# Feed-forward of the first block: six more pairs of the first linear in seven block products, 19 of 22 per layer

## What is computed

```python
def conv_ffn(h, in_w, conv_w, conv_b, out_w):
    u = causal_dwconv(h @ in_w, conv_w, conv_b)   # in_w 1024 x 5632, conv of width 3 over positions
    g, v = jnp.split(u, 2, axis=-1)
    return (jax.nn.silu(g) * v) @ out_w           # out_w 2816 x 1024
```

## Time and profile before

| | |
|---|---|
| median of 3 runs | 3198.08 us |
| profiled execution | 3200.7 us |
| its span, first to last instruction | 3198.9 us |
| TensorE busy, share of the span | 3125.3 us, 98% |
| VectorE busy | 1258.0 us, 39% |
| ScalarE busy | 704.9 us, 22% |
| GpSimd busy | 283.4 us, 9% |
| granted TensorE clock, mean | 0.994 |

### The profile page before, as it was taken

The page is one execution under the profiler, slowest core; times in us unless marked ns, Lnnn a source line. Parts: engine busy times, 40 slices in busy tenths (PEclk is TensorE's granted clock), DMA queues, the critical chain, the costliest instruction groups (busy, mean ns, idle before and its releaser), DMA issues.

```text
span 3198.9 us, 44256 instructions
## 1 busy us (share of the span) xinstructions
PE 3125.3 (98%) x18040; PEld 2426.9 (76%) x18040; DVE 1258.0 (39%) x2669; ACT 704.9 (22%) x1252; POOL 283.4 (9%) x240
## 2 busy tenths in 40 slices
PE   8999999999999999999999999999999999999998
PEld 7788899988899888998799988888454455544544
DVE  4622278463478445753357543431211111111111
ACT  3621121252221152102211132420111111111111
POOL 0210011070010100001100013200000000000000
PEclk9999999999999999999999999999999999999999
DMA  6543344433244433443244443235899999999996
GB/s 241 158 145 132 119 158 172 158 119 119 89 176 160 154 119 132 171 164 140 93 179 166 150 158 119 80 133 206 341 428 428 429 429 427 429 429 429 428 429 261
DMA packets 72432, 719.51 MB, mean 225 GB/s; under 512 B 8112, under 2 KB 8112, under 8 KB 10336
## 3 DMA queue, kind: packets, MB, share of 16 engines
q1 hardware_dynamic: 70416, 710.06, 56.0%
q0 software_dynamic: 1872, 7.38, 1.0%
HBM read 716.32 MB, written 1.08 MB: 224 GB/s over the span
## 4 chain that ended last, share of the span: by engine, by line
PE 85%; DMA 9%; DVE 4%; ACT 1%; issue 1%; POOL 0%; SPq 0%; DVEq 0%; POOLq 0%; ACTq 0%
PE bank L285 30%; PE bank L2393 11%; PE bank L3466 10%; DMA weight_ring<-in_experts 9%; PE bank L304 9%; PE bank L1392 8%; PE bank L3497 5%; PE bank L3451 3%; PE bank L3443 2%; PE bank L2691 1%; DVE residual L1137 1%; PE bank L1244 0%; PE bank L1224 0%; PE bank L487 0%; PE bank L1691 0%
## 5 line engine op out<-in xcount | busy, mean ns | idle before, releaser
L285 PE MATMUL bank<-normed_residual,weight_ring 128*128 128x256 f32 x2592 | 577.6, 381 | 0.0
L285 PEld LDWEIGHTS bank<-normed_residual,weight_ring 128*128 128x128 f32 x2592 | 488.9, 190 | 72.6 <-issue 8.7
L285 PE MATMUL bank<-arena,weight_ring 128*128 128x256 f32 x1368 | 303.6, 382 | 4.7 <-ACT arena L1751 3.9
L285 PEld LDWEIGHTS bank<-arena,weight_ring 128*128 128x128 f32 x1368 | 261.3, 192 | 41.6 <-issue 4.8
L3550 DVE TENSOR_TENSOR arena<-bank,arena 128x512 f32<-128x512 f32 x32 | 22.1, 692 | 615.7 <-PE bank L3466 615.7
L3466 PE MATMUL bank<-weight_ring,arena 128*64 128x512 f32 x1024 | 227.7, 593 | 3.1 <-DMA weight_ring<-in_experts 3.1
L3466 PE MATMUL bank<-arena 128*64 128x512 f32 x1024 | 226.6, 595 | 2.7 <-DVE arena L3544 2.7
L304 PE MATMUL bank<-gained_residual,weight_ring 128*128 128x256 f32 x896 | 205.0, 389 | 23.9 <-DVE gained_residual L378 12.0
L3497 PE MATMUL bank<-weight_ring,arena 128*64 128x512 f32 x992 | 219.7, 595 | 0.0
L304 PEld LDWEIGHTS bank<-gained_residual,weight_ring 128*128 128x128 f32 x896 | 174.4, 195 | 51.2 <-DVE gained_residual L378 14.0
L3466 PEld LDWEIGHTS bank<-weight_ring,arena 128*64 128x64 f32 x1024 | 72.5, 137 | 153.0 <-issue 139.0
(11 more groups left out here) (449 smaller groups left out, 4220.3 us busy)
## 6 DMA issues: line engine op xcount, KB each, us to landing
weight_ring<-in_stream SPq DMA_DIRECT2D x290, 1024.0 KB, 4.8
weight_ring<-in_experts SPq DMA_DIRECT2D x126, 2048.0 KB, 18.6
arena<-in_experts SPq DMA_DIRECT2D x66, 2048.0 KB, 18.9
arena<-rows POOLq DMA_DIRECT2D x8, 512.0 KB, 6.7
residual<-in_x SPq DMA_DIRECT2D x1, 1024.0 KB, 4.9
arena<-in_mem POOLq DMA_DIRECT2D x1, 1024.0 KB, 5.3
out<-gained_residual SPq DMA_DIRECT2D x4, 256.0 KB, 2.7
constants<-in_con SPq DMA_DIRECT2D x1, 612.5 KB, 7.2
```

Source lines behind the costliest of these rows:

```text
L285: mm = nc.tensor.matmul(PB[b][:, m * T:m * T + T], l, r, start=(kc == 0), stop=(kc == chunks - 1))
```

## The change

The condition `p % 3 != 2` goes, so pairs 5, 8, 11, 14, 17 and 20 of the first linear are in block products too, in both layers: 19 of 22 pairs in place of 13. All that follows from the list (order, step numbers, buffers by turns) changes with it. The PSUM banks of the pairs, the stream of weights and the second linear stay.

```diff
 def through_blocks(name, p):
 
-    return name[:6] == "ffn_in" and p > 2 and p % 3 != 2 or name[:7] == "ffn_out" and p < FFN_OUT_WHOLE
+    return name[:6] == "ffn_in" and p > 2 or name[:7] == "ffn_out" and p < FFN_OUT_WHOLE
```

## The result

The changed kernel takes 3210.01 us (median of 10 runs, 3207.65 to 3212.56) against 3200.37 us for the kernel before (median of 10 runs on the same occasion, 3197.57 to 3203.54). The ratio is 1.0028, 95% interval 1.0020 to 1.0036: slower, by 9.6 us between the medians. The forecast was 3205.9 us, which is 7.8 us more than the median known then; that median was of 3 runs and has moved up by 2.3 us with seven more. The profiled execution took 3209.6 us, its span is 3207.8 us.

The account below looks back on a forecast made before the run. VectorE's sums for the second linear's second block were taken to set the feed-forward's end: 3.9 us later per layer, +7.8 us in both, 3198.1 + 7.8 = 3205.9 us. The 8-in-10 range was 3199.0 to 3209.5 us.

Parts of the forecast that it names:

- The place: VectorE's sums for the second linear's second block set the feed-forward's end; they come 3.9 us later per layer.
- The sum: VectorE's priced work from putting pair 4 together to those sums: 123.4 us, ending at 550.3 against 546.4.
- putting together: VectorE assembling a block (L1465 on) in the first linear: 1.71 us each, 18 of them 30.8 us.
- a pair: One first-linear pair in blocks needs 5.92 us of VectorE without collision, against TensorE's 6.25 us.
- ten collisions: GpSimd's multiplication meeting VectorE's sums, 1.08 us each: ten per layer instead of seven, 10.7 us.
- waits of VectorE: VectorE's waits for TensorE in this stretch, 24.3 us on record before, were to vanish almost entirely.
- TensorE's waits: TensorE waits for VectorE from pair 16 into the second linear: 8.3 us per layer.
- the 0.5 us that was there before: TensorE's existing wait for VectorE's last sum (L1438) where the second linear begins, 0.54 us on record.
- Rival 1: VectorE does not fill up; without collisions TensorE sets the feed-forward's end: 3.3 us earlier per layer, 3191.5 us, chance 0.07.
- Rival 2: The three new collisions do not come in the first linear: 3199.4 us, no difference, chance 0.13.
- Rival 3: Repeated waits in TensorE's stream lower its clock: at 0.98 in this stage 5 us more, 3211 us, chance 0.05.
- The rule of the Trainium skill: VectorE operations with two SBUF inputs and GpSimd's SBUF reads block each other fully: 0.5 us more per layer at 1.26 us each.

Follow-up runs that it names:

- e5: Kernel before, with VectorE's taps moved ahead of the putting together: 3199.41 us against 3201.07, ratio 0.9994.
- e1: Changed kernel with GpSimd's multiplication cut from 512 columns to 8 of one tile (result incomplete): 3195.95 us against 3202.15 for the kernel before, ratio 0.9981.
- e2: Changed kernel with VectorE's taps moved ahead of the putting together, everything computed: 3196.22 us against 3202.15 for the kernel before, ratio 0.9981.
- e3: Kernel before with only the early pairs 5, 8 and 11 added in block products (16 of 22): 3195.73 us against 3202.15, ratio 0.9979.
- e7: Changed kernel timed once more, unaltered: 3210.89 us against 3201.07 for the kernel before, ratio 1.0031.
- e6: e2's kernel, with the second linear's second-block sums also ahead of pair 21's taps: 3191.89 us against 3201.07 for the kernel before, ratio 0.9972.

## Why the prediction was right

**The place.** The prediction said that the end of the feed-forward is set by the sums of the second linear's second block, and that their shift is the change's whole effect. They ended (L1453 behind them) at 548.80 with a stage begun at 412.94, 135.86 us into it; before at 546.41 and 414.35, 132.06 us. The shift is 3.8 us, the forecast 3.9.

**The sum.** Its terms held one by one: putting together 1.71 us, sums 2.52 us, a pair 5.92 us and with a collision 7.00 us, ten collisions of ten, waits of VectorE 24.3 us down to 0.2. The taking of prices from start to start and the check on the kernel before (546.4 against 546.41) is what made a difference of 4 us between sums of 120 us usable.

**TensorE's waits.** All came in the forecast pairs, the first in pair 16. On record they are shorter than forecast (0.74 in pair 16 for 0.8, 1.68 for 2, 1.94 for another 2, 0.56 for 0.8), and those of pairs 20 and 21 carry no bracket. The starts show them: in pair 20 the 4 matmuls from 523.73 take 0.89 us and the next piece begins at 524.93, 0.3 us behind them, and in pair 21 it is 0.2 us. These two and the short records of the others are the difference between 6.3 us on record and 8.3 us by starts. The forecast of 8.3 us holds, though its last term, the 0.5 us that was there before, was 0.7 to 0.8 by starts (e5).

**The rivals.** Rival 1 (faster, if the collisions went) did not happen, but e1 made its condition true, e2 all but one collision of it, and both got its result: -3.2 and -3.5 us per layer, forecast -3.3. Rival 2 (the three new ones do not come) fell with ten multiplications of 1580 ns. Rival 3 fell with a clock of 1.00 in a stage with gaps.

**The rule of the Trainium skill** ("SBUF — State Buffer", "Who interferes with whom") is borne out by e2: operations with at most one input in SBUF run beside the multiplication at their own length, and it at its own. Its "fully blocks" would have been 1.26 us a collision; measured is 1.08 (1.75 us for an operation of 0.68). By the starts in the earlier trace rows the next sum stood at 444.06 and the multiplication's record ends at 443.68 + 1.58 = 445.26, 1.20 us later, so the sum had only the rest of the multiplication to wait for. That the loss is under the whole length for this reason is argued, not tested.

**What was off.** The total came to 9.6 and 9.8 us in two comparisons where the mechanism gives 7.6. Each interval holds 7.6, and the other kernels' medians deviate from their stages to both sides (e3 gained 2.5 us more than its stages, e2 1.1 us less). Whether the 2 us belong to the change is open. If they do, they lie outside the forecast's terms, which stop at the feed-forward.

## What to carry to other kernels

When work is moved from a full engine to one that is 76% busy, do not compare shares: add up the second engine's time from start to start between two fixed points, and set the added work against the waits that lie between them, since waits behind the last point that someone waits at, or too far ahead of it, pay for nothing. Steps that look like slack for one engine may be what keeps two others apart: the whole pairs gave VectorE time to catch up and gave GpSimd's multiplication a place beside operations it does not disturb. Where a trace shows two engines lengthening each other's operations, put the one's operation beside work of the other that it leaves alone, in the order by hand; here that turned 9.8 us lost (e7) into 9.2 us gained (e6) with the same instructions.

## What the runs showed of the hardware

The collision costs both sides. GpSimd's multiplication began 0.22 us into a sum of VectorE and took 1.58 us in place of 1.26, and the next sum took 1.75 us in place of 0.68 while the sum that was running kept its 0.68. Read from these lengths, GpSimd gets in between two operations of VectorE that stand in line. The 8-column multiplication of e1 shows the first half alone: it took 0.51 us beside the sums and 0.19 us where it met none, and the sum behind it kept its 0.69 us. The one that met none:

```profile
885.00 0.19 POOL L1653 TENSOR_TENSOR arena<-arena 128x8 f32<-128x8 f32 x1 [15.17 <-DVE arena L1573]
```
